# State-space tables loaded on the slabs' queue with two buffers; at each new x the last output slab summed in one region, its first blocks made by VectorE, and a high part moved

## What is computed

```
# first block, l = 0, 1
mod = silu(c) @ w_ada[l] + b_ada[l]              # shift_a, scale_a, gate_a, shift_m, scale_m, gate_m
h = rms_norm(x, g_pre_mix[l]) * (1 + scale_a) + shift_a
y = concat([mlstm(h), rms_norm(window_attention(h), g_attn_out[l])]) @ w_out[l]
x = x + gate_a * rms_norm(y, g_post_mix[l])
h = rms_norm(x, g_pre_mlp[l]) * (1 + scale_m) + shift_m
y = square(relu(h @ w_up[l])) @ w_down[l]        # width 8192 between
x = x + gate_m * rms_norm(y, g_post_mlp[l])
# second block
u, z = split(rmsnorm(h, g_pre) @ s5_w_in)
y = gelu(s5_ssm(u, a, log_dt, b, c, d));  y = y * sigmoid(y @ s5_w_glu + b_glu) * silu(z)
h = h + rmsnorm(y @ s5_w_out, g_post)
k, v, f = rmsnorm(h, g_kv) @ kv_w;  q, z = split(rmsnorm(h, g_pre) @ fox_w_in)
h = h + rmsnorm((fox_attention(q, k, v, f) * silu(z)) @ fox_w_out, g_post)
```

## Time and profile before

| | us |
|---|---|
| median of 3 runs | 3237.44 |
| the runs | 3237.97, 3228.82, 3237.44 |
| the profiled execution, its time | 3234.48 |
| its span | 3232.6 |
| its mean granted TensorE clock | 0.986 |
| PE busy in it | 3096.2 (96%) |
| DVE busy | 2518.7 (78%) |
| ACT busy | 1567.5 (48%) |

### The profile page before, as it was taken

The page is one execution under the profiler, slowest core; times in us unless marked ns, Lnnn a source line. Parts: engine busy times, 40 slices in busy tenths (PEclk is TensorE's granted clock), DMA queues, the critical chain, the costliest instruction groups (busy, mean ns, idle before and its releaser), DMA issues. The chain is left out here.

```text
span 3232.6 us, 49521 instructions
## 1 busy us (share of the span) xinstructions
PE 3096.2 (96%) x20336; PEld 2691.0 (83%) x20336; DVE 2518.7 (78%) x3174; ACT 1567.5 (48%) x2348; POOL 0.2 (0%) x4
## 2 busy tenths in 40 slices
PE   4899999999999999999999999999998899999998
PEld 3788778888888888888888888888887788888887
DVE  7997999798988888777987666789669677656765
ACT  2455654444444566765534444445443456434454
POOL 0000000000000000000000000000000000000000
PEclk7999999999999999999999999999999999999999
DMA  9777869988888645554687666776554553654453
GB/s 409 303 302 302 320 248 343 336 336 332 340 331 336 237 181 208 207 220 146 248 315 264 238 206 227 262 268 239 217 174 170 181 184 135 227 185 157 145 190 109
DMA packets 136978, 790.27 MB, mean 244 GB/s; under 512 B 20081, under 2 KB 38897, under 8 KB 46001
## 3 DMA queue, kind: packets, MB, share of 16 engines
q1 hardware_dynamic: 108002, 754.65, 63.2%
q10 hardware_dynamic: 28752, 32.45, 3.1%
HBM read 769.28 MB, written 17.76 MB: 243 GB/s over the span
## 5 line engine op out<-in xcount | busy, mean ns | idle before, releaser
L1535 DVE TENSOR_TENSOR wl<-raw,wh 128x2048 fp32r<-128x2048 f32 (+1 forms) x484 | 1097.4, 2267 | 235.0 <-ACT wh L888 234.5
L403 PE MATMUL bk<-HX,wh 128*128 128x512 f32 x4592 | 1117.1, 396 | 4.5 <-ACT wh L888 3.0
L403 PEld LDWEIGHTS bk<-HX,wh 128*128 128x128 f32 x4592 | 845.5, 189 | 178.5 <-ACT wh L888 3.6
L888 ACT ACTIVATE wh<-raw 128x2048 fp32r<-128x2048 f32 x479 | 913.7, 1908 | 31.8 <-DMA raw<-in_w_in 26.1
L403 PEld LDWEIGHTS bk<-HX,wl 128*128 128x128 f32 x4592 | 571.2, 188 | 31.3 <-DVE wl L1535 8.8
L403 PE MATMUL bk<-HX,wl 128*128 128x256 f32 x4592 | 579.1, 278 | 3.7 <-DVE wl L1535 3.7
L403 PE MATMUL bk<-hb,wh 128*128 128x512 f32 x2048 | 492.1, 392 | 2.7 <-ACT hb L888 2.4
L1543 DVE SCALAR_TENSOR_TENSOR raw<-raw,cb 128x2048 f32<-128x2048 f32 x192 | 437.5, 2285 | 14.9 <-DMA raw<-in_w_ada 14.9
L403 PEld LDWEIGHTS bk<-hb,wh 128*128 128x128 f32 x2048 | 375.3, 188 | 78.5 <-ACT hb L888 3.2
L403 PEld LDWEIGHTS bk<-hb,wl 128*128 128x128 f32 x2048 | 256.4, 189 | 12.1 <-DVE wl L1535 1.6
L403 PE MATMUL bk<-hb,wl 128*128 128x256 f32 x2048 | 259.1, 279 | 0.8 <-DVE wl L1535 0.8
(11 more groups left out here) (299 smaller groups left out, 2706.1 us busy)
## 6 DMA issues: line engine op xcount, KB each, us to landing
raw<-in_w_ada SPq DMA_DIRECT2D x192, 1024.0 KB, 5.8
raw<-in_w_up SPq DMA_DIRECT2D x128, 1024.0 KB, 5.6
raw<-in_w_down SPq DMA_DIRECT2D x128, 1024.0 KB, 5.2
raw<-in_w_in SPq DMA_DIRECT2D x68, 1024.0 KB, 5.3
raw<-in_kv_w SPq DMA_DIRECT2D x33, 1024.0 KB, 4.8
raw<-in_w_out SPq DMA_DIRECT2D x32, 1024.0 KB, 4.8
raw<-in_s_w_in SPq DMA_DIRECT2D x32, 1024.0 KB, 4.8
raw<-in_fox_w_in SPq DMA_DIRECT2D x32, 1024.0 KB, 4.8
```

The lines of the kernel that those rows point to most:

```text
L403: return e.matmul(o_, l_, r_, start=start, stop=stop, skip_group_check=True)
L888: return e.activation(o_, i_, f, **kw)
L1535: return e.tensor_tensor(o_, a_, b_, op)
```

## The change

At a turn: (1) the last output slab adds both halves in one region of the bank, by 32 matmuls of 128x256 in place of 16 of 128x512; `half` and `joined` of it are gone. At i = 0, 2, 4, 5 ACT squares straight from the bank and then copies `yt` out; at i = 1, 3 one DVE add makes `yt`. (2) ACT makes rsy before the gated square `ts[:, 2]`. (3) DVE makes blocks 0 and 1 of `sq` itself (`first_two`), from `xs` = X * scale, which ACT prepares a slab earlier; X itself is updated for these two later. (4) `high` of slab +20 stands at the end of `to_h`, ahead of the `hb` instructions. (5) 82 tiles start one slab later, and the two tiles after slabs 3 and 4 of the layer-1 input move by one.

For the tables: the parameters' steps move from n = 14, 15, 18 to 19, 21, 25 and the transposes from m = 16 to 22. The 12 `btg` loads and the `bq`, `ah` loads are issued by SP between the slabs' loads; `ah`, `bq` and `abt` get two buffers, and their slabs are spaced in pairs (`AB_AT`).

At the end of the layer-1 mixer the gain of `qa` is folded into DVE's scaling (eight of 128x256), and `out_gate`, `m_gated` of the last slab stand behind `next_high`, `next_low`.

```diff
+AB_AT = [90 + 3 * (q // 2) + q % 2 for q in range(15)] + [113]
+
+XN_AT = {2: 1, 3: 2, 4: 5, 5: 6}
...
-          31, 32, 33, 33, 35, 36] + list(range(37, 51)) + spread(J_MLP[0] + 3, J_MLP[0] + 110, 82)
-         + [J_IN[1] + n for n in (3, 4, 10, 15, 16, 18, 19, 24, 25, 29, 30, 31, 32, 33)]
+          31, 32, 33, 33, 35, 36] + list(range(37, 51)) + spread(J_MLP[0] + 4, J_MLP[0] + 110, 82)
+         + [J_IN[1] + n for n in (4, 5, 10, 15, 16, 18, 19, 24, 25, 29, 30, 31, 32, 33)]
...
+                one = j - 15 in TURNS
                 for q, k in enumerate(order):
+                    if one:
+                        for part in range(2):
+                            mm(bank[:, 0:T], WH[w][:, k, :], x(k)[:, part, :], q == 0 and part == 0, False)
+                        continue
                     if first:
...
-                if m == 16:
+                if m == 22:
...
-                if j in SPLIT:
+                if j in SPLIT and j - 19 not in TURNS[:-1]:
                     high(SPLIT[j])
...
+                if n == 15:
+                    return
...
-                if i in (1, 3):
-                    e.wait_ge(s_yt, 24 * (i - 1) + 32 + n + 1)
+                g, by = gg[:, n:n + 1], 1.0 if i < 4 else 0.25 if i == 4 else 0.5
+                last = n == 15 and i not in (1, 3)
+                if n < 15 and i in (1, 3):
+                    e.wait_ge(s_yt, 47 * (i // 2) + 32 + n + 1)
+                elif not last:
+                    e.wait_ge(s_ev, TURNS[i] + n + 1)
                 else:
-                    e.wait_ge(s_ev, TURNS[i] + n + 1)
+                    e.wait_ge(s_slab, TURNS[i] + n + 1)
                 if n >= 4:
                     e.wait_ge(s_yadd, 14 * i + n - 3)
-                act(ts[:, 0, :], y, ACT.Square).then_inc(s_ysq, 1)
-                if i < 5:
-                    act(ts[:, 2, :], y, ACT.Square, scale=gg[:, n:n + 1]).then_inc(s_y2, 1)
+                if last:
+                    ps = BK[BANK_OF[TURNS[i] + n]][:, 0:T]
+                    act(ts[:, 0, :], ps, ACT.Square, scale=by).then_inc(s_ysq, 1)
+                    if i < 5:
+                        e.wait_ge(s_t1, 16 * i + 14)
+                    act(y, ps, ACT.Copy, scale=by).then_inc(s_ev, 1)
+                    e.wait_ge(s_ev, TURNS[i] + n + 1)
+                else:
+                    act(ts[:, 0, :], y, ACT.Square).then_inc(s_ysq, 1)
                 if n == 15:
                     y_rms(i)
-                act(YU[:, n, :], y, ACT.Copy, scale=gg[:, n:n + 1]).then_inc(s_yg, 1)
+                if i < 5:
+                    act(ts[:, 2, :], y, ACT.Square, scale=g).then_inc(s_y2, 1)
+                act(YU[:, n, :], y, ACT.Copy, scale=g).then_inc(s_yg, 1)
                 if n == 13:
                     log_and_exp()
                 if n == 14 and i < 5:
                     high(TURNS[i] + 19)
+                    s = scale_of(i)
+                    for k in range(2):
+                        act(XS[i][:, k, :], X[:, k, :], ACT.Copy, scale=s[:, k:k + 1]).then_inc(s_x01, 1)
...
-                for g, q in enumerate(GROUPS):
+            def to_h(i, shift=None):
+
+                scale = scale_of(i)
+
+                for g, q in list(enumerate(GROUPS))[2:]:
                     if g == 4:
                         e.wait_ge(s_sx, i + 1)
                         rsqrt(RS[:, :], SX[:, :], D, LN[i][:, :], s_rx)
-                    e.wait_ge(s_xn, 6 * i + g + 1)
+                    e.wait_ge(s_xn, 6 * i + XN_AT[g])
...
+                high(TURNS[i] + 20)
...
-                    for k in range(4 * g, 4 * g + 4):
-                        c = PER_LAYER * l + G_ATT + k
-                        last = act(QA[:, k, :], QA[:, k, :], ACT.Copy, scale=PRM[:, c:c + 1])
-                    last.then_inc(s_ag, 1)
-                    e.wait_ge(s_ag, 2 * l + g + 1)
+                    if l == 0:
+                        for k in range(4 * g, 4 * g + 4):
+                            c = PER_LAYER * l + G_ATT + k
+                            last = act(QA[:, k, :], QA[:, k, :], ACT.Copy, scale=PRM[:, c:c + 1])
+                        last.then_inc(s_ag, 1)
+                        e.wait_ge(s_ag, g + 1)
...
-                        if n < 3 and m == b + 2 + 3 * g:
-                            if u:
-                                e.wait_ge(s_k0m, u)
-                            e.dma_start(BTG[:, :, :, :], d["s5_bt"][4 * g:4 * g + 4].rearrange("q p r n -> p q r n")
-                                        ).then_inc(s_bt, 16)
...
-                    if m == 90 + 2 * q:
-                        e.wait_ge(s_atk, 16)
-                        e.wait_ge(s_cc, 128)
-                        if q:
-                            e.wait_ge(s_ab, q)
-                        e.dma_start(BQ[:, :, :], d["s5_b"][q]).then_inc(s_abl, 16)
-                        for w in range(4):
-                            e.dma_start(AH[32 * w:32 * w + 32, :, :].rearrange("p a r s -> p (a r s)"),
-                                        at_keep[4 * q + w:4 * q + w + 1, :].to_broadcast([32, 768])).then_inc(s_abl, 16)
-                    if m == 92 + 2 * q:
+                    if m == AB_AT[q] + 1:
                         e.wait_ge(s_ab, q + 1)
-                        e.dma_start(ab_keep[q], ABT[:, :, :, :]).then_inc(s_abk, 16)
+                        e.dma_start(ab_keep[q], ABT[q % 2][:, :, :, :]).then_inc(s_abk[q % 2], 16)
...
+                    if l and n == N_IN - 1:
+                        out_gate(l, 5)
...
+                def first_two():
+                    s = scale_of(i)
+                    for k in range(2):
+                        tmp = XT[i][:, k, :]
+                        settled(tt(tmp, YU[:, k, :], rsy, ALU.mult))
+                        e.wait_ge(s_x01, 2 * i + k + 1)
+                        stt(SQ[:, k, 0:T], tmp, s[:, k:k + 1], XS[i][:, k, :], ALU.mult, ALU.add).then_inc(s_xh, 1)
+
+                if i < 5:
+                    first_two()
                 for g, q in enumerate(GROUPS):
                     if g == 4 and i < 5:
+                        tt(X[:, 0:2, :], X[:, 0:2, :], XT[i][:, :, :], ALU.add).then_inc(s_xn, 2)
                         x_squares()
-                    renewed(g, q)
+                    if g > 1 or i == 5:
...
-                    tt(QA[:, q, :], QA[:, q, :], bc(ARS[:, :], 4), ALU.mult).then_inc(s_qn, 1)
+                    if l == 0:
+                        last = tt(QA[:, q, :], QA[:, q, :], bc(ARS[:, :], 4), ALU.mult)
+                    else:
+                        for k in range(4 * g, 4 * g + 4):
+                            c = PER_LAYER * l + G_ATT + k
+                            last = stt(QA[:, k, :], QA[:, k, :], PRM[:, c:c + 1], ARS[:, :], ALU.mult, ALU.mult)
+                    last.then_inc(s_qn, 1)
...
+                if j == 3 and n == 15:
+                    i = 2 * l + 1
+                    e.wait_ge(s_slab, down_slab(l, j, n) + 1)
+                    e.wait_ge(s_yg, 16 * i + 14)
+                    e.wait_ge(s_t1, 16 * i + 14)
+                    tt(yt, BK[BANK_OF[down_slab(l, j, n)]][:, 0:T], y, ALU.add).then_inc(s_ev, 1)
+                    return
...
-                if n == 14:
+                if n == 19:
...
-                if n == 15:
+                if n == 21:
...
-                if n == 18:
+                if n == 25:
...
-                    if n == 91 + 2 * q:
-                        e.wait_ge(s_abl, 80 * (q + 1))
+                    if n == AB_AT[q]:
+                        ah, bq, abt = AH[q % 2], BQ[q % 2], ABT[q % 2]
+                        e.wait_ge(s_abl[q % 2], 80 * (q // 2 + 1))
+                        if q:
+                            e.wait_ge(s_ab, q)
...
+                for u in range(12):
+                    n, g = divmod(u, 4)
+                    if j == J_MLP[1] + 44 + 16 * n + 3 * g:
+                        if u:
+                            e.wait_ge(s_k0m, u)
+                        e.dma_start(BTG[:, :, :, :], d["s5_bt"][4 * g:4 * g + 4].rearrange("q p r n -> p q r n")
+                                    ).then_inc(s_bt, 16)
+                for q in range(16):
+                    if j == J_MLP[1] + AB_AT[q] + 4:
+                        e.wait_ge(s_atk, 16)
+                        e.wait_ge(s_cc, 128)
+                        if q >= 2:
+                            e.wait_ge(s_ab, q - 1)
+                        e.dma_start(BQ[q % 2][:, :, :], d["s5_b"][q]).then_inc(s_abl[q % 2], 16)
+                        for w in range(4):
+                            e.dma_start(AH[q % 2][32 * w:32 * w + 32, :, :].rearrange("p a r s -> p (a r s)"),
+                                        at_keep[4 * q + w:4 * q + w + 1, :].to_broadcast([32, 768])
+                                        ).then_inc(s_abl[q % 2], 16)
```

More of the change, by code:

```diff
@@ L146 @@
 for _j in range(N_SLABS):
-    _n += not any(_t + 16 <= _j < _t + 16 + SIDE for _t in TURNS[:-1])
+    _n += not any(_t + 15 <= _j < _t + 16 + (_t < TURNS[-1]) * SIDE for _t in TURNS)
```

(23 more changed lines are left out.)

53 lines of the change are left out of this document (31 added, 22 removed).

## The result

The changed kernel took 3215.12 (median of 4 runs, 3212.46 to 3219.95), the one before 3237.7 (4 runs, 3228.82 to 3238.56): a ratio of 0.9937, 95% interval 0.9917 to 0.9958, that is 20 us less, between 14 and 27 (the two medians lie 22.6 apart). The forecast was 3220, 3212 to 3231. The profiled execution took 3216.80, against 3234.48 before and the 3218.6 of the sum. One execution of experiment 4 took 3990.05 at a granted clock of 0.724 and is left out of its median.

The account below looks back on a forecast made before the run. PE, busy for 96% of the span, bounds the kernel, so only places where it stands still or runs at half clock pay. The terms sum to -15.9, 3221.5 from the median; the forecast was 3220, range 3212 to 3231.

Parts of the forecast that it names:

- PE has `tacc` to sum, so the shorter chain starts nothing earlier: Turn 0: 0.87 leaves ACT's chain, but PE, busy with `tacc`, can use the square only 0.17 earlier.
- Side passes 1.2 later: Turn 0: with the gated square after `ln` and rsy, side passes begin 3.80 after `ln`, 1.2 later than before.
- The narrow matmuls: Last slab of a turn: 32 matmuls of 128x256 for 16 of 128x512 add 0.2.
- the six turns: Turns 0 to 5 together: -0.3, from -1.0, +0.25, -0.6, +0.7, +1.1 and -0.7.
- `wh` ahead of `hb`, the tile later: 2.3 back at turn 0: First two slabs behind turn 0: no `wh` wait and no late low part, so they cost 2.3 less.
- Turn 1: The side passes' delay is swallowed by a later wait for DVE; DVE's added work costs +0.25.
- End of the mixer: Layer-1 mixer's end: `wh` can start 0.8 earlier, half clock may go, `mx` may be waited for; -1.2.
- S5 parameters: Slab with the S5 parameters: moving their DVE blocks removes a wait of 2.15 and half clock; -4.2.
- `ah`, `bq`: Table steps: SP issues the DMAs in ACT's place, two slabs at 0.75 each; -1.5.
- Last turn: Turn without xy or side passes: 0.87 less in the chain, 0.2 more in the matmuls; -0.7.
- `btg`: Three late `btg` loads, moved to SP: waits of 5.2 and two clock falls of 1.7 go; -8.7.
- The rival of the clock at the turns: New PE waits of 1.6 at five turns make the clock fall, 1.7 each, 8.5 together: 3228; chance 0.17.

Follow-up runs that it names:

- experiment 4: Changed kernel with ACT making the gated square `ts[:, 2]` ahead of `ln` and rsy at the turns; 3210.43, ratio 0.9927.
- experiment 1: The changed kernel run again with no edit; 3213.18, ratio 0.9936.
- Experiment 10: Changed kernel with `wh` of slab +20 back behind the first `hb` instructions; 3214.84 (one run).
- experiment 6: The kernel before, run again unedited for its trace; 3230.81 (one run).
- experiment 7: The kernel before with only the 12 `btg` loads moved to SP; 3226.3 (10 runs), ratio 0.9978.
- experiment 5: Changed kernel with the 12 `btg` loads back on ACT's queue behind the `c_keep` stores; 3213.59, ratio 0.9937.
- experiment 3: Changed kernel with its edits at the turns undone, plus 32 small unread matmuls at the start of PE's list; 3216.79, ratio 0.9954.

## Why the prediction was right, and where not

- **PE has `tacc` to sum, so the shorter chain starts nothing earlier.** Right in kind. PE used the square 0.33 earlier, not 0.17: the rows' durations include the overlap with the next, and start to start the `tacc` sums take 1.29, not 1.45.
- **Side passes 1.2 later.** Mis-sized: 0.64 from the `tacc` sums, where it had 1.0. The same error stands in it again. I added durations (the unread matmuls 1.46; start to start 1.29), so behind `ln` it is 1.02 for 1.2; and `ln` begins 0.38 sooner behind the `tacc` sums (1.98 for 2.36), where I had 0.17. The narrow matmuls, put at 0.2, cost 0.1 or less. Undisturbed, the six turns gave 3.5 where the sum had 0.3.
- **`wh` ahead of `hb`, the tile later: 2.3 back at turn 0.** It was 2.2 in the trace of experiment 1. Experiment 10 shows 1.25 of it to be the move of `wh`.
- **Turn 1.** The added DVE work was to cost 0.25; it gained 0.6, since the side passes began only 0.15 later and the small waits behind them went. The wait for DVE's low part grew from 1.05 to 1.39, as foreseen in kind.
- **End of the mixer, -1.2 within 0 and -2.8.** -2.0 or -0.5, by the clock. The wait for `mx` that the prediction named came.
- **S5 parameters, -4.2.** -4.2. **`ah`, `bq`, -1.5.** -1.5. **Last turn, -0.7.** -0.9.
- **`btg`, -8.7.** The trace of before cannot bear that number as a fixed cost. The waits, 5.2, are fixed in that kernel; the 3.4 for the clock are not (experiment 6). Alone the step gives about 7 (experiment 7). As a part of the whole it is 0.4 by the medians and 0.8 or 2.6 by the account, since on ACT the loads would now have landed up to 2.7 sooner and been waited for 1.8 (experiment 5). The Trainium skill's rule of rings that are taken in order ("DMA: Bandwidth & Descriptors", "Queues, rings and completion order") agrees with the landings: 14.0 to 17.6 behind the stores on ACT's ring, at most 9.5 on SP's. The other rule, that issuers share the engines, would have left the term near nothing, and it was 7. But SP also issues the load 0.4 to 0.7 ahead of the stores, where ACT issued it behind them, so no run here separates the ring from the order in time.
- **The rival of the clock at the turns.** A wait of 1.41 to 1.47 (1.6 forecast) stood in the sums at five turns of seven traces, and the clock fell once in these 35 places, where a late load had put a wait of 1.22 just ahead.
- **Not foreseen:** 2.7 to 3.8 in the S5 outputs. The prediction lists the places where PE stands still or runs at half clock, and leaves this one out, though the trace of before has 11.6 of stops and a clock of 0.84 in its 63.7 us (experiment 3). The change does nothing there, so the gain is luck as far as the forecast goes. In the profiled execution it makes up for the late load at turn 0, 2.4 off its term. So part of the agreement of the total, 3216.80 for 3218.6, is errors that cancel.

## What to carry to other kernels

Work out a chain on an in-order engine from start to start, not by durations: pipelined rows overlap, and five rows gave an error of 0.5 us a turn. Before a step is given a price, ask which part of it is a wait and which is the clock behind it; the second comes and goes between executions of the same kernel, so look at two traces. An engine that is freed hands its time to the next in line: here ACT's order and the unread matmuls cost 1.6 and 1.3 a turn, and DVE let 0.5 of either through at turns 0 and 2, and 1.3 to 1.6 at turn 4.

## What was not expected of the hardware

- PE's stops for "issue" in a dense run of small matmuls lie at other places when other instructions stand ahead, and with 64 rows more at the start of the program a stretch 2400 us later took 3.9 us less (experiment 3). What the stops are, the profile does not show. One such kernel is little to go by, and two executions of the kernel before differ by 2.0 there; in its favour stand the means of the other traces on either side.
- Behind waits of the same place and length the clock falls in one execution and not in another: behind 1.93 in five of nine, behind 2.04 in one of two. Behind 1.47 alone it never did, at 34 places. The prediction took the 3.12 of layer 0 as a place where it does not fall; in the changed kernel it fell there both times (3.61 and 3.47 for 2.10) and cost nothing, since a wait for the low part behind it went.
- Each product with `btg` cost 0.2 more in some executions: behind the last first-of-group product the changed kernel's first trace lost 0.7 against before, its second nothing. No view here shows why.
